# Retention in a two-block latent network: pairs of heads, turned outputs, the mean taken off on TensorE

## The reference, cut to what matters

```python
def step(s, qkv):                      # chunks of 128 tokens; o_f and o_b are added
    scores = einsum('bihd,bjhd->bhij', qc, kc) * intra_decay
    o = einsum('bhij,bjhe->bihe', scores, vc) + einsum('bihd,bhde->bihe', qc, s) * q_decay
    s = s * chunk_decay + einsum('bjhd,bjhe->bhde', kc * k_decay, vc)
...
o_lf starts from the state that the context leaves, o_cf from zero (o_lb, o_cb the same, reversed)
def ret_out(o, g):                     # per token and head, over the 64 values
    return (o - mean(o)) * rsqrt(mean((o - mean(o)) ** 2) + EPS) * silu(g)
y = concatenate([attention, ret_out]) @ w_out
```

## Time and profile before

| | us |
|---|---|
| median of 3 runs | 2784.44 (2782.74 to 2785.47) |
| profiled execution, device time | 2778.06 |
| its span | 2776.3 |
| PE busy | 2485.9 (90%) |
| DVE busy | 771.8 (28%) |
| ACT busy | 352.8 (13%) |
| mean granted clock of TensorE | 0.939 |

### The profile page before, as it was taken

One profiled execution on the slowest core, in us unless ns is written; L12 is line 12 of the kernel. 1 busy time (PEld: TensorE's weight loads), 2 busy tenths in 40 slices (PEclk: granted clock), 3 DMA queues, 4 the chain that ended last, 5 costly groups with the idle time before them and its releaser, 6 DMA issues.

```text
span 2776.3 us, 26691 instructions
## 1 busy us (share of the span) xinstructions
PE 2485.9 (90%) x11097; PEld 1580.8 (57%) x11097; DVE 771.8 (28%) x1520; ACT 352.8 (13%) x756; POOL 187.1 (7%) x357
## 2 busy tenths in 40 slices
PE   6998876898999994188999999889999999889998
PEld 3445555443444443147846874557865884566873
DVE  2145434228556214702200001242002000342002
ACT  2122311100111004211000000131001000131000
POOL 1000000210445400000001000000000000000000
PEclk8999965999999997599999999999999999999999
DMA  7456500221445325253445443505444444514443
GB/s 242 151 172 220 166 29 15 70 84 61 152 137 171 118 76 173 104 178 114 145 154 183 152 144 129 165 31 166 152 141 151 152 146 148 152 50 137 153 146 111
DMA packets 278319, 370.71 MB, mean 134 GB/s; under 512 B 24555, under 2 KB 216647, under 8 KB 273463
## 3 DMA queue, kind: packets, MB, share of 16 engines
q1 hardware_dynamic: 260832, 332.75, 37.1%
q0 software_dynamic: 15456, 35.06, 3.9%
q10 hardware_dynamic: 1910, 1.20, 0.2%
HBM read 344.84 MB, written 22.02 MB: 132 GB/s over the span
## 4 chain that ended last, share of the span: by engine, by line
PE 85%; DVE 9%; issue 2%; DMA 2%; ACT 2%; SPq 0%; DVEq 0%; ACTq 0%
PE banks L201 73%; PE banks L1299 1%; PE banks L1163 1%; PE banks L1136 1%; DMA weights<-in_ada_w 1%; PE banks L1286 1%; PE banks L1152 1%; PE banks L2599 1%; DMA weights<-in_w_in 1%; PE banks L475 1%; DMA weights<-s_from 0%; PE banks L536 0%; PE banks L2572 0%; PE banks L1743 0%; DVE statistics L1177 0%
## 5 line engine op out<-in xcount | busy, mean ns | idle before, releaser
L201 PE MATMUL banks<-h_columns,weights 128*128 128x256 f32 (+1 forms) x3840 | 950.1, 410 | 10.1 <-issue 7.9
L201 PEld LDWEIGHTS banks<-h_columns,weights 128*128 128x128 f32 x3840 | 733.3, 191 | 213.6 <-issue 124.4
L201 PE MATMUL banks<-weights,big 128*128 128x512 f32 (+2 forms) x2112 | 716.3, 523 | 84.1 <-ACT big L842 54.9
L201 PEld LDWEIGHTS banks<-weights,big 128*128 128x128 f32 (+2 forms) x2112 | 318.8, 183 | 461.7 <-issue 371.4
L201 PE MATMUL banks<-weights,h_columns 128*128 128x512 f32 (+4 forms) x960 | 376.3, 550 | 21.9 <-issue 14.1
L201 PEld LDWEIGHTS banks<-weights,h_columns 128*128 128x128 f32 x960 | 183.8, 194 | 199.7 <-issue 157.5
L2148 DVE TENSOR_TENSOR big<-normed_rows,banks 128x256 f32<-128x256 f32 x88 | 37.0, 421 | 562.5 <-PE banks L201 562.5
L1809 POOL DMA_DIRECT2D s_inside<-kernel_lags x256 | 127.5, 507 | 46.7 <-ACT statistics L1793 44.3
L2162 POOL DMA_DIRECT2D row_vectors<-in_ln_g x6 | 3.3, 554 | 1573.6 <-DVE statistics L2204 1033.1
L2174 DVE SCALAR_TENSOR_TENSOR x_rows<-banks,x_rows 128x512 f32<-128x512 f32 x24 | 16.6, 692 | 317.2 <-PE banks L201 317.2
L2134 ACT ACTIVATE normed_rows<-banks 128x256 f32<-128x256 f32 x88 | 33.8, 384 | 550.2 <-PE banks L201 550.2
(11 more groups left out here) (407 smaller groups left out, 1724.5 us busy)
## 6 DMA issues: line engine op xcount, KB each, us to landing
weights<-in_mlp_w SPq DMA_DIRECT2D x64, 1024.0 KB, 5.4
weights<-in_ada_w SPq DMA_DIRECT2D x48, 1024.0 KB, 7.3
weights<-in_ffn_w_gate SPq DMA_DIRECT2D x44, 1024.0 KB, 5.3
weights<-in_ffn_w_up SPq DMA_DIRECT2D x44, 1024.0 KB, 5.3
weights<-in_ffn_w_down SPq DMA_DIRECT2D x32, 1024.0 KB, 5.0
weights<-in_w_out SPq DMA_DIRECT2D x12, 1024.0 KB, 5.1
weights<-in_ffn_w_down SPq DMA_DIRECT2D x16, 768.0 KB, 4.4
weights<-in_w_in SPq DMA_DIRECT2D x16, 768.0 KB, 4.4
```

Source lines behind the costliest of these rows:

```text
L201: ins = T.engine.matmul(out, lhsT, rhs, start=start, stop=stop)
```

## The change

1. Heads go in pairs p (two heads m = 0, 1). The score matmuls of the two heads alternate (rows 0 to 63 and 64 to 127 of the array), each into its own bank.
2. The product with the values is turned: the values are stationary (64 columns), the decayed scores move (256 columns), and the output comes with channels on partitions, head m on partitions 64m to 64m+63 of bank 4. The state's part is added in the same accumulation, with decayed queries (one multiplication on VectorE for each pair).
3. The copied sums are multiplied with a centring matrix (identity less 1/64 in each head's block), which takes off the mean and turns back to rows in bank 5. ScalarE squares it, VectorE sums, ScalarE takes the root, VectorE scales and gates one pair (512 columns); then it is transposed into `hT`. All of it runs for pair p-1 beside the scores and sums of pair p.
4. The exponents of the decays, their exp, the decayed keys and the states move into the attention's steps: for all heads the exponents at t = 2 and the exp at t = 3; for h of 4 and more the decayed keys at t = 1 and state matmuls with their copy at t = 2; at h = 7 two exps of the query decays in each step.
5. Silu of the gate moves to the start of the retention. The first part of the output product (16 of its 64 matmuls, those that need the attention alone and the first 512 columns) goes around the last pair's centring and transposes, ahead of the residual gate's rows.
6. A constant of 256 KB is loaded at the start on GpSimd's queue, and VectorE builds the centring matrix and copies the log decays there.

```diff
+        for m in range(2):
+            half, other = slice(RD * m, RD * (m + 1)), slice(RD * (1 - m), RD * (2 - m))
+            V.engine.tensor_scalar(self.centre[half, half], self.ident[half, half], -1.0 / RD, None, ALU.add)
+            V.engine.memset(self.centre[half, other], 0.0)
...
+                if t == 2 and h >= 4:
+                    self.tensor_retention_state(T, h - 4)
...
+                if t == 1 and h >= 4:
+                    self.vector_decayed_keys(V, h - 4)
+                if t == 2:
+                    self.vector_decay(V, h)
+                if t == 2 and h >= 4:
+                    self.vector_retention_state(V, h - 4)
...
+                if t == 3:
+                    self.scalar_decay(A, h)
+                if h == H - 1:
+                    self.scalar_decay_of_queries(A, t)
...
+    def vector_decayed_keys(self, V, p):
+        e = V.engine
+        for t in range(2):
+            o = MLA_IN + RET_W + P * p
+            k = self.z[:, TL + t, o:o + P].rearrange("p (h d) -> p h d", d=RD)
+            for c in range(2):
+                w = self.dec[:, 2 + t, 2 * p:2 * p + 2, c].unsqueeze(2).to_broadcast([P, 2, RD])
+                ins = e.scalar_tensor_tensor(self.decayed_keys()[:, t, c].rearrange("p (h d) -> p h d", d=RD), k, RD ** -0.5, w,
+                                             ALU.mult, ALU.mult)
+        ins.then_inc(self.sem("decayed_keys"), 1)
+        V.engine.wait_ge(self.sem("decayed_keys"), V.due("decayed_keys"))
...
+    def tensor_retention_state(self, T, p):
...
+        for c in range(2):
+            for t in range(2):
+                for m in range(2):
+                    half = slice(RD * m, RD * (m + 1))
+                    ins = T.engine.matmul(self.ps[half, 6, c * RD:(c + 1) * RD], self.decayed_keys()[:, t, c, half],
+                                          self.rv(TL + t, 2 * p + m), start=t == 0, stop=t == 1)
...
+    def scalar_decay_of_queries(self, A, p):
+        for c in range(2):
+            ins = A.engine.activation(self.decay_of_queries(p)[:, c, :], self.lengths[:, c, :], ACT.Exp,
+                                      scale=self.lg_pairs[:, p, c:c + 1])
+        ins.then_inc(self.sem("query_decays"), 1)
+        A.engine.wait_ge(self.sem("query_decays"), A.due("query_decays"))
...
+    def tensor_retention_scores(self, T, p):
+        q, k = self.turned_of(p, 0), self.turned_of(p, 1)
+        T.engine.wait_ge(*T.freed(6))
+        T.engine.wait_ge(*T.freed(7))
+        for g in range(2):
+            for m in range(2):
+                T.engine.wait_ge(*T.freed(2 * m + g))
+            for j in range(2):
+                tok = slice((2 * g + j) * P, (2 * g + j + 1) * P)
+                for m in range(2):
+                    half = slice(RD * m, RD * (m + 1))
+                    ins = T.engine.matmul(self.ps[:, 2 * m + g, j * N_LAT:(j + 1) * N_LAT], k[half, tok],
+                                          q[half, g * N_LAT:(g + 1) * N_LAT], start=True, stop=True)
+            ins.then_inc(self.sem("psum_for_vector"), 1)
+            T.hand([g, 2 + g], "vector")
+    def tensor_retention_sums(self, T, p):
+        T.engine.wait_ge(*T.freed(4))
+        for g in (1, 0):
+            T.engine.wait_ge(self.sem("decayed_scores"), 2 * p + 2)
+            for j in range(2):
+                for m in range(2):
+                    half = slice(RD * m, RD * (m + 1))
+                    ins = T.engine.matmul(self.ps[half, 4, g * N_LAT:(g + 1) * N_LAT], self.rv(2 * g + j, 2 * p + m),
+                                          self.w_of(m, g)[:, j, :], start=j == 0, stop=g == 1 and j == 1)
+            for c in range(2) if g == 0 else ():
+                for m in range(2):
+                    half = slice(RD * m, RD * (m + 1))
+                    ins = T.engine.matmul(self.ps[half, 4, 0:N_LAT], self.state_of(p)[half, c, :],
+                                          self.decayed_queries(p)[half, c, :], start=False, stop=c == 1)
+        ins.then_inc(self.sem("psum_for_scalar"), 1)
+        T.hand([4], "scalar")
+    def tensor_retention_rows(self, T, p):
+        T.engine.wait_ge(*T.freed(4))
+        T.engine.wait_ge(*T.freed(5))
+        for t in range(TT):
+            ins = T.engine.matmul(self.ps[:, 5, t * P:(t + 1) * P], self.ro_columns[:, p % 2, t * P:(t + 1) * P],
+                                  self.centre[:, :], start=True, stop=True)
+        ins.then_inc(self.sem("centred"), 1)
+        T.hand([5], "vector")
+    def tensor_retention_out(self, T, p):
+        T.engine.wait_ge(self.sem("retention_rows"), T.due("retention_rows"))
+        T.engine.wait_ge(*T.freed(5))
+        for t in range(TT):
+            ins = T.engine.transpose(self.ps[:, 5, t * P:(t + 1) * P], self.ro_rows[:, p % 2, t, :], self.ident[:, :])
+        ins.then_inc(self.sem("psum_for_scalar"), 1)
+        T.hand([5], "scalar")
+    def tensor_retention(self, T):
+        self.tensor_retention_turn(T, 0)
+        for p in range(H // 2):
+            self.tensor_retention_scores(T, p)
+            if p + 1 < H // 2:
+                self.tensor_retention_turn(T, p + 1)
+            if p:
+                self.tensor_retention_rows(T, p - 1)
+            self.tensor_retention_sums(T, p)
+            if p:
+                self.tensor_retention_out(T, p - 1)
+    def vector_retention_turn(self, V, p):
+        V.engine.wait_ge(self.sem("psum_for_vector"), V.due("psum_for_vector"))
+        q = self.turned_of(p, 0)
+        V.engine.tensor_copy(q, self.ps[:, 6, :]).then_inc(self.sem("vector_released"), 1)
+        V.engine.wait_ge(self.sem("vector_released"), V.due("vector_released"))
+        V.engine.wait_ge(self.sem("query_decays"), V.due("query_decays"))
+        V.engine.tensor_tensor(self.decayed_queries(p), q[:, 0:N_LAT].unsqueeze(1).to_broadcast([P, 2, N_LAT]),
+                               self.decay_of_queries(p), ALU.mult).then_inc(self.sem("vector_step"), 1)
+        V.engine.wait_ge(self.sem("vector_step"), V.due("vector_step"))
...
+    def vector_retention_rows(self, V, p):
+        e, rows = V.engine, self.ro_rows[:, p % 2].rearrange("p t (h d) -> p t h d", d=RD)
+        m2 = self.sm[:, 192 + 8 * p:200 + 8 * p]
+        V.engine.wait_ge(self.sem("centred_squares"), V.due("centred_squares"))
+        e.tensor_reduce(m2, self.xn[:, 2048:2560].rearrange("p (m d) -> p m d", d=RD), AX.X, ALU.add)\
+            .then_inc(self.sem("vector_step"), 1)
+        V.engine.wait_ge(self.sem("vector_step"), V.due("vector_step"))
+        self.vector_rsqrt(V, m2, m2, 1.0 / RD, EPS)
+        e.tensor_tensor(rows, self.ps[:, 5, :].rearrange("p (t h d) -> p t h d", t=TT, d=RD),
+                        m2.rearrange("p (t h) -> p t h", t=TT).unsqueeze(3).to_broadcast([P, TT, 2, RD]), ALU.mult)\
+            .then_inc(self.sem("vector_released"), 1)
+        if p == 0:
+            V.engine.wait_ge(self.sem("retention_gate"), V.due("retention_gate"))
+        o = MLA_IN + 3 * RET_W + P * p
+        rows = self.ro_rows[:, p % 2]
+        e.tensor_tensor(rows, rows, self.z[:, :, o:o + P], ALU.mult).then_inc(self.sem("retention_rows"), 1)
...
+    def vector_retention(self, V):
+        self.vector_retention_turn(V, 0)
+        for p in range(H // 2):
+            self.vector_retention_scores(V, p)
+            if p + 1 < H // 2:
+                self.vector_retention_turn(V, p + 1)
+            if p:
+                self.vector_retention_rows(V, p - 1)
+        self.vector_retention_rows(V, H // 2 - 1)
...
+    def scalar_retention_rows(self, A, p):
+        A.engine.wait_ge(self.sem("centred"), A.due("centred"))
+        A.engine.activation(self.xn[:, 2048:2560], self.ps[:, 5, :], ACT.Square).then_inc(self.sem("centred_squares"), 1)
+        A.engine.wait_ge(self.sem("centred_squares"), A.due("centred_squares"))
+        self.scalar_root(A, self.sm[:, 192 + 8 * p:200 + 8 * p])
...
+        for p in range(H // 2):
+            if p + 1 < H // 2:
+                self.scalar_retention_turn(A, p + 1)
+            if p:
+                self.scalar_retention_rows(A, p - 1)
+            self.scalar_retention_sums(A, p)
+            if p:
+                self.scalar_retention_out(A, p - 1)
+        self.scalar_retention_rows(A, H // 2 - 1)
+        self.scalar_retention_out(A, H // 2 - 1)
...
+        slots.append(self.tile_begins(T))
+        part(0, 0)
+        self.tensor_retention_rows(T, last)
+        for t in (1, 2):
+            part(0, t)
+        self.tensor_retention_out(T, last)
+        part(0, 3)
         self.tensor_gate(T, 0, 2, 2, [4, 5, 6, 7])
         self.tensor_needs_hT(T)
+        for n in range(1, 4):
+            slots.append(self.tile_begins(T))
+            for t in range(TT):
+                part(n, t)
```

More of the change, by code:

```diff
@@ L1258, in tensor_retention @@
+    def tensor_retention_state(self, T, p):
         T.engine.wait_ge(self.sem("decayed_keys"), T.due("decayed_keys"))
-        T.engine.wait_ge(self.sem("z_from_scalar"), T.due("z_from_scalar"))
+        if p == 0:
```

(62 more changed lines are left out.)

213 lines of the change are left out of this document (63 added, 150 removed).

## The result

| | before | changed |
|---|---|---|
| median, us | 2783.59 (2782.23 to 2785.47, 4 runs) | 2704.43 (2702.89 to 2708.89, 4 runs) |
| profiled execution, us | 2778.06 | 2705.52 |
| mean granted clock | 0.939 | 0.955 |

The ratio is 0.9722, interval 0.971 to 0.9735, some 77 us less (the two medians lie 79.2 apart). I had forecast 2728 with 2709 to 2750.

A forecast was written before the change was run, and what follows sets the result against it. TensorE, busy 90% of the span, was taken as the bound, losing time in the 171.8 us stage after the attention. That stage becomes 108.6, 63.2 less; minus 6 and 0.8 gives 56.4 less: 2728 us, range 2709 to 2750.

The forecast's parts named there:

- The opening, the periods, the pairs: Retention's new pair loop: opening and four pairs priced at 36.8 us at full clock, 59.7 at half.
- The clock: TensorE's clock in the new pair loop: a mixture of full and half, rather more full, was taken.
- The 48: Time in us taken for the four pairs with opening, between 36.8 at full clock and 59.7 at half.
- my two arguments for the full clock: Pair loop: paired matmuls fill both array halves and the time; matmuls after dense small ones (L1265, L1311) run at full speed.
- Why the halves matter: Pair loop: matmuls in different array halves overlap, a pair priced as one matmul; rival without overlap 2754 us, chance 0.10.
- my 7.5 at the upper end: State's four matmuls in the sums: if not overlapping, 3.9 to 7.5 us more; 7.5 kept in the range.
- The moved work: Decays, decayed keys and state matmuls moved into the attention: 6 us more (4 to 8).
- the sign that I had set: Attention: a head slower at h below 4 would show the prediction wrong; the 6 us should lie in heads 4 to 7.
- The start: Kernel's start: one more transfer of 256 KB, 0.8 us more (0 to 1).
- After the pairs: From the pairs to the output product's end: product, last centring, transposes, gate rows and changes of form, 60.6 us.
- The likeliest case: Pair loop at a mixture of clocks: 56.4 us less, 2728 us (own range 2717 to 2739), chance 0.52.
- the rival with 0.18: Clock stays up in the pair loop, pairs at VectorE's pace: 69.9 us less, 2714.5 us, chance 0.18.

The follow-up runs named there:

- run 8: Changed kernel with two more VectorE passes over 1664 elements in each pair's rows, ahead of the sum of squares; 2731.16 us in its one run.
- run 5: Changed kernel with the last pair's centring and transposes directly behind each other and the whole output product behind the gate rows; 2714.45 us, ratio 0.9754.
- run 12: run 9's kernel (retention values wrong) with TensorE kept idle 9 us ahead of the pairs, so that they are entered at half clock; 2730.7 us, one run.
- run 6: Kernel before with the value product alone turned, heads one by one, nothing turned back (result partly wrong); 2759.61 us, ratio 0.9922.
- run 7: Changed kernel with both heads' value products written to the same partitions, forbidding overlap in the sums (values wrong); 2708.57 us, ratio 0.9727.
- run 1: Changed kernel with a pair's two heads one after the other, not alternating, in scores, sums and state's part; 2705.68 us, ratio 0.9725.
- run 2: Changed kernel with four VectorE passes between attention and retention, TensorE waiting about 9 us and entering the pairs at half clock; 2718.13 us in its one run.
- run 4: Kernel before with only the decay matrices' exponents and exp moved into the attention's steps; 2780.92 us, ratio 0.9994.
- run 9: Changed kernel with the value product turned back to sixteen 64-column matmuls a pair, decayed scores as weights (values wrong); 2714.98 us, ratio 0.9753.

## Why the prediction was wrong

Taken from profiled execution to profiled execution, 56.4 us were forecast and 72.5 measured.

1. *The opening, the periods, the pairs* at full clock were 1.8, 7.6, 9.6, 9.6, 8.2 (36.8); measured 1.8, 7.3, 9.4, 9.3, 7.8 (35.6). The prices of scores (2.0), sums with state (2.9, measured 3.0), turns, centring, and VectorE's chain as what sets the period were right.
2. *The clock* is the step that failed. "I take a mixture, rather more full than half ... 48": it was 1.00 from the first pair to the last. 12.4 of the 16 us missed are this term. The 48 was no term worked out from rows but the middle of two cases (36.8 and 59.7). The reason I gave against the full clock, TensorE's gaps of 1 to 2 us in each pair, was wrong: the gaps of 1.4 cost nothing here, while those of 4.6 to 5.2 in run 8, and the 3.75 with its neighbours in run 5, brought it down. The length of a gap isn't the whole of it, for run 12 fell back with none above 1.34. And the head loop of before was no precedent: it lay at half clock because of what it issued (run 6). Of my two arguments for the full clock, the halves filled by pairs aren't needed (run 6 has them unfilled, run 7 in the sums); and that matmuls ran at full speed after L1265 is so, but not after L1311, behind which TensorE was idle for 20 us. What exactly in the new loop holds the clock up stays open, and so does how long a gap it stands there.
3. *Why the halves matter* was wrong in its weight. The overlap exists, without alternation too (run 1), in the state's part as well (1.08 us for four, so my 7.5 at the upper end was not needed); taking it from the sums costs 0.2 in pairs 1 and 2, where VectorE sets the period, and 1.7 in pairs 0 and 3 (run 7): 3.9 in all, and none of it by the clock. The paired scores' overlap was never taken away, so what it is worth was not measured.
4. *The moved work* was to cost 6 and "all in heads 4 to 7". The attention grew by 4.5 (169.55 us against 165.06, from the modulation row that starts at 197.67 and before at 198.01). The state matmuls take 0.69 a pair at full clock, and head 4 grew by 1.4, the wait for the bank included, as reckoned. 2.7 us lie in heads 1 to 3, and come from windows at half clock (0.90 over each of these heads), not from the exponents (run 2 has these too, at 1.00 and 17.18 a head). Such dips differ between executions of much the same attention: run 6, with the attention of before, took 18.2 for head 1. So the sign that I had set, "a head of the attention slower at h below 4", came true for a reason that says nothing about the exponents; what sets them off stays open.
5. *The start* was to cost 0.8 and cost nothing: the input stage ended 0.3 us earlier.
6. *After the pairs* 60.6 were forecast and 60.0 measured. The cover of the last rows by the first quarter of the product I priced at 4 "without that cover"; it is 9 (run 5): 5.4 of idle time and 2.8 of gate rows at half clock, with some 0.6 less plain.
7. *The median.* I took off its 6.4 us above the profiled execution unchanged. The changed kernel's median lies 1.1 below its own profiled one, so a further 5 to 7 us came from there. For the profiled execution alone, the sum with the clock up gives 2778.1 - 69.9 = 2708.2, and 2705.5 was measured.

The likeliest case was wrong; the rival with 0.18 was right, and the range was too narrow for it together with the spread of the runs.

Where the stage's 76.1 us come from, as far as it was shown: about 22 are the clock in the head loop (run 6), 9 the product around the last rows (run 5), none the early decays alone (run 4). The remainder, some 45, I put down to the 9.1 of the opening, for which the attention pays part of its 4.5, to the norm and the state's part running beside the pairs in place of VectorE's 25 us at the end, and to the pairs' shorter scores; the trace shows where this time went, but these were not tried apart.

## What to carry to other kernels

A stage's clock is a term of the sum like any other: before you take it from the old loop, ask what the new one issues (whole weights for 64 columns, as run 6 shows; gaps like the 5.2 us of run 8), and where it isn't plain, forecast two numbers and not their mean. Filling idle times of TensorE, like the 5.4 us around the last rows in run 5, with work from the next stage can pay twice, for the time and for the speed of what follows. And a single profiled execution can lie 6 us off its own median; compare it with a spread before carrying the difference over.

## What the runs showed of the hardware

- Half-array float32 matmuls overlap even when two of the same half follow each other: eight scores of 256 columns in 2.10 us against 2.00 with strict alternation (run 1).
- Four matmuls from both row halves into one bank, each to its own half of the partitions, took 1.08 us, where one costs 0.49: they overlap. The Trainium skill, "TensorEngine Tiling (Array Packing)", Restrictions and Gotchas, would have had them one after the other; the measurement decides.
- Eight 64-column matmuls with a 128x128 weight each cost as much as four of 256 columns with 64 columns of weights: 3.68 us for either group at half clock, and at full clock 3.76 for sixteen (run 9) against 1.94 for four (run 6).
- A loop with TensorE busy 16.0 of 19.0 us stayed at 0.50; with its value product turned (run 6) its granted clock rose from 0.50 (380 to 390) to 0.85 (396 to 406) and 0.98 (406 to 416).
